# Seven block products in place of eight in the gate/up part of both feed-forward layers

## The reference, cut to what matters

```python
D_FF = 2816                                 # ((8 * 1024 + 3 * 256 - 1) // (3 * 256)) * 256

def swiglu(h, w_gate_up, w_down):
    gu = h @ w_gate_up                      # (tokens, 1024) @ (1024, 5632)
    g, u = gu[..., :D_FF], gu[..., D_FF:]
    return (jax.nn.silu(g) * u) @ w_down    # (tokens, 2816) @ (2816, 1024)

x = x + mix
x = x + swiglu(rms_norm(x, norm_ffn_g[i]), w_gate_up[i], w_down[i])
```

## Time and profile before

| | |
|---|---|
| device time, median of 3 runs | 1802.62 us (1800.88 to 1804.29) |
| the profiled execution | 1802.11 us |
| its span | 1800.4 us |
| mean granted TensorE clock | 0.997 of full |
| PE busy | 97% |
| VectorE busy | 46% |
| ScalarE busy | 34% |
| GpSimd busy | 2% |

### The profile page before, as it was taken

How to read it: one execution, slowest core, us unless ns; L and a number is a source line. 1 busy time by engine, 2 the same in 40 slices (tenths; PEclk the granted TensorE clock), 3 DMA queues, 4 the chain that set the end, 5 groups by cost and what they waited for, 6 DMA issues and landing times.

```text
span 1800.4 us, 33060 instructions
## 1 busy us (share of the span) xinstructions
PE 1747.0 (97%) x14564; PEld 1622.8 (90%) x14564; DVE 827.6 (46%) x975; ACT 610.6 (34%) x887; POOL 28.1 (2%) x51
## 2 busy tenths in 40 slices
PE   7999999999999999999999998999899999999999
PEld 7999666689999999999999995666899999999999
DVE  6663366664433333334532327777544423442333
ACT  5443355553221122112342206666442211221221
POOL 0000000000000000000000000000000000000000
PEclk9999999999999999999999999999999999999999
DMA  5225799921222222112223339998122222122122
GB/s 187 74 96 205 288 378 381 376 101 65 94 70 71 74 91 70 71 71 72 92 94 129 129 118 373 374 375 318 71 71 72 92 71 71 70 72 93 71 70 82
DMA packets 38436, 258.42 MB, mean 144 GB/s; under 512 B 4528, under 2 KB 4656, under 8 KB 9264
## 3 DMA queue, kind: packets, MB, share of 16 engines
q1 hardware_dynamic: 34560, 245.15, 36.7%
q0 software_dynamic: 3760, 11.54, 1.8%
HBM read 242.51 MB, written 13.11 MB: 142 GB/s over the span
## 4 chain that ended last, share of the span: by engine, by line
PE 89%; DVE 5%; ACT 3%; issue 2%; DMA 0%; SPq 0%; ACTq 0%; DVEq 0%
PE ps L412 62%; PE ps L212 4%; PE ps L213 4%; PE ps L214 4%; PE ps L768 3%; PE ps L672 2%; PE ps L719 2%; PE ps L688 2%; PE ps L455 2%; PE ps L701 1%; PE ps L676 1%; PE ps L739 1%; DVE pw L1035 1%; ACT sp L892 1%; DVE st L1055 1%
## 5 line engine op out<-in xcount | busy, mean ns | idle before, releaser
L412 PE MATMUL ps<-h_hi,w_hi 128*128 128x320 f32 x1664 | 380.1, 310 | 2.6 <-DVE qks L1277 1.1
L412 PE MATMUL ps<-h_hi,w_lo 128*128 128x320 f32 x1664 | 379.2, 309 | 0.0
L412 PE MATMUL ps<-h_lo,w_hi 128*128 128x320 f32 x1664 | 379.0, 309 | 0.0
L190 DVE TENSOR_TENSOR w_lo<-w_raw,w_hi 128x2048 fp32r<-128x2048 f32 x99 | 226.8, 2291 | 154.1 <-ACT w_hi L182 144.3
L412 PEld LDWEIGHTS ps<-h_hi,w_hi 128*128 128x128 f32 x1664 | 278.2, 188 | 3.7 <-DVE w_lo L190 2.5
L412 PEld LDWEIGHTS ps<-h_lo,w_hi 128*128 128x128 f32 x1664 | 278.2, 188 | 0.0
L182 ACT ACTIVATE w_hi<-w_raw 128x2048 fp32r<-128x2048 f32 x99 | 188.7, 1906 | 263.7 <-PE ps L412 263.5
L412 PEld LDWEIGHTS ps<-h_hi,w_lo 128*128 128x128 f32 x1664 | 278.0, 188 | 0.0
L212 PE MATMUL ps<-w_hi,h_hi 128*128 128x256 f32 x640 | 183.0, 286 | 11.8 <-DVE h_lo L243 10.6
L213 PE MATMUL ps<-w_lo,h_hi 128*128 128x256 f32 x640 | 181.8, 284 | 0.0
L214 PE MATMUL ps<-w_hi,h_lo 128*128 128x256 f32 x640 | 181.7, 284 | 0.0
(11 more groups left out here) (186 smaller groups left out, 2098.2 us busy)
## 6 DMA issues: line engine op xcount, KB each, us to landing
w_raw<-in_w SPq DMA_DIRECT2D x99, 1024.0 KB, 4.8
kv<-in_k_s SPq DMA_DIRECT2D x30, 1024.0 KB, 8.2
kv<-in_v_a SPq DMA_DIRECT2D x18, 1024.0 KB, 7.9
work<-in_v_s SPq DMA_DIRECT2D x16, 1024.0 KB, 8.8
kv<-in_k_a SPq DMA_DIRECT2D x14, 1024.0 KB, 8.6
work<-in_v_a SPq DMA_DIRECT2D x14, 1024.0 KB, 8.8
extra<-in_k_a SPq DMA_DIRECT2D x8, 1024.0 KB, 7.4
w_raw<-in_k_a SPq DMA_DIRECT2D x8, 1024.0 KB, 8.9
```

The costliest lines, as they stand in the source:

```text
L190: nc.vector.tensor_tensor(w_lo[s][:, :, :], w_raw[:, s, :, :], w_hi[s][:, :, :].bitcast(F32), ALU.subtract).then_inc(lo_done, 1)
L412: last = nc.tensor.matmul(ps[:, bank0 + 2 * n + h, 0:HALF], w[:, k, n * P:(n + 1) * P], m[:, k, h * HALF:(h + 1) * HALF], start=(k == 0 an ...
```

## The change

Both feed-forward layers compute gate and up of one block with Strassen's algorithm in Winograd's form. The factors are taken as 2 x 2 blocks: the tokens in two halves, the 8 input tiles as 4 pairs of an even and an odd tile, the outputs as gate and up. Seven products of 4 input tiles by 320 tokens by 128 outputs replace eight. A product is 4 x 3 = 12 matmuls of the size used before, and a unit 84 of them in place of 96. The down units are as before.

The operands of the products are sums of blocks. On the token side they are made once per layer (class `PairNorm`: ScalarE, VectorE, and on GpSimd `difference` and `add`, which also sums the squares). On the weight side three of the seven are blocks of `w_raw` and four are sums, which GpSimd makes for every unit (`factor13`, `factor4`). The high and low parts of the seven are made one by one (`gu_hi_block`, `gu_lo_block`), each as soon as the product before that used its buffer is done. The results are combined through three PSUM banks a unit: a bank is read, and then a further product is accumulated onto it. GpSimd also takes three of the elementwise operations behind a unit. The loops of the feed-forward layers are written out.

```diff
+            def begin(i):
+                pe.wait_ge(lo_done, split_count(g, j, i))
+                if i < 3:
+                    if v > 1:
+                        pe.wait_ge(ff[("g0", "c21", "c12")[i]], v - 1)
+                else:
+                    pe.wait_ge(ff[("p1", "u2", "p5", "u3")[i - 3]], v + 1)
+            def product(i, pairs):
+                (w1, w0), (m1, m0) = (s_hi[i], s_lo[i]), combos(i)
+                for p in pairs:
...
+                    for a, (w, m) in enumerate(((w1, m1), (w1, m0), (w0, m1))):
+                        last = nc.tensor.matmul(ps[:, bank[i], 0:HALF], w[:, p, :], m[:, p, :],
+                                                start=(i < 3 and p == 0 and a == 0), stop=(p == 3 and a == 2),
...
+            def factor13(g, j, v):
+                raw_ready(pool, g, j, j % 2)
+                if v > 0:
+                    pool.wait_ge(lo_done, gu_split(v - 1, 4))
...
+                nc.gpsimd.tensor_tensor(out, b0[:, 512:1536], b0[:, 0:1024], ALU.subtract).then_inc(ff["t"], 1)
+                pool.wait_ge(ff["t"], 3 * v + 1)
+                nc.gpsimd.tensor_tensor(t2[:, :, :], raw_block(j % 2, 2), t13[:, 0], ALU.subtract)\
...
+                    if j > 0:
+                        gate_half(v + j - 1, 1 - s)
+                    if j + 1 < n:
+                        factor4(g, j + 1, v + j + 1)
+                    if j > 0:
+                        scale(v + j - 1, 1 - s)
+                    up_half(v + j, s)
+                    if j + 2 < n:
+                        factor13(g, j + 2, v + j + 2)
...
+                    copy_p1(act, v + j, s)
+                    if more:
+                        gu_hi_block(act, g, j + 1, 0)
+                    if j > 0:
+                        silu(v + j - 1, 1 - s)
+                    if more:
+                        gu_hi_block(act, g, j + 1, 1)
+                    copy_p5(v + j, s)
+                    if more:
+                        gu_hi_block(act, g, j + 1, 2)
+                        gu_hi_block(act, g, j + 1, 3)
+                    else:
+                        split_hi(act, d, 0, 0, (prod, 7 * (v + n) - 3))
+                    if j > 0:
+                        split_gu(v + j - 1, j - 1)
...
+            def u3(v, s):
+                dve.wait_ge(prod, 7 * v + 5)
+                nc.vector.tensor_tensor(up[:, s, HALF:TOK], ps[:, 3 * s + 1, 0:HALF], p1[:, s, :], ALU.add)\
...
+                    if more:
+                        gu_lo_block(dve, g, j + 1, 0)
+                    u2(v + j, s)
+                    if more:
+                        gu_lo_block(dve, g, j + 1, 1)
+                        gu_lo_block(dve, g, j + 1, 2)
+                    if j > 0:
+                        product(v + j - 1, 1 - s)
+                    g0(v + j, s)
+                    if more:
+                        gu_lo_block(dve, g, j + 1, 3)
+                    u3(v + j, s)
+                    if not more:
+                        split_lo(dve, d, 0, 0)
+                    else:
+                        gu_lo_block(dve, g, j + 1, 4)
+                    if j > 0:
+                        split_gu(v + j - 1, j - 1)
+                    c12(v + j, s)
+                    if more:
+                        gu_lo_block(dve, g, j + 1, 5)
+                    c21(v + j, s)
+                    if more:
+                        gu_lo_block(dve, g, j + 1, 6)
```

More of the change, by code:

```diff
@@ L157, in program, with layer @@
         settled = sem("settled")
[L160 to L164, removed]
+        def layer(f):
+            for c, n in enumerate(CHUNKS):
+                yield from ((f"g{f}{c}", n, 0, 7), (f"d{f}{c}", 4, 2, 1))
+        order = [("qkv", 12, TT, 1), ("oa", 4, 2, 1), *layer(0), ("ks", 4, 2, 1), ("vs", 4, TT, 1), ("qb", 4, 2, 1),
+                 ("ob", 4, 2, 1), *layer(1)]
+        units, splits, u0, m0 = {}, [], 0, 0
+        for name, n, per, parts in order:
+            l0 = splits[-1] if splits else 0
+            units[name] = (u0, m0, per, l0, parts)
+            splits += [l0 + parts * (j + 1) for j in range(n)]
             u0, m0 = u0 + n, m0 + n * per
@@ L436, in program @@
         x_done = sem("x_done")
[L438 to L445, removed]
+        OUT = (6, 4)
         def output_pe(pe, ph, x0, ready, ready_s, mid=None):
-            pe.wait_ge(lo_done, units[ph][0] + 1)
+            pe.wait_ge(lo_done, split_count(ph, 0))
             for h in range(2):
@@ new lines, in pair_act, with pair_dve, chunks @@
+        def pair_act(f):
+            nm = norms[f"ffn{f}"]
+            return lambda act, j: nm.pair_act(act, j, (lambda: copy_p1(act, f * N_F, 0)) if j == 3 else None)
+        def pair_dve(norm):
+            return lambda dve, j, n: norm.odd_dve(dve, j) if n else norm.even_dve(dve, j)
+        ff = sems("ff", "t p1 p5 u2 u3 g0 c12 c21 c22 g1 silu sr gu hi lo")
+        prod = sem("prod")
+        N_F = sum(CHUNKS)
+        def chunks(f):
+            v = f * N_F
+            for c, n in enumerate(CHUNKS):
+                yield c, n, f"g{f}{c}", f"d{f}{c}", v
+                v += n
@@ new lines, in ffn_pe @@
+        def ffn_pe(pe, f, x0, nm):
+            for c, n, g, d, v in chunks(f):
+                for j in range(n):
+                    gu_unit(pe, g, j, v + j, nm if c == 0 and j == 0 else None)
+                v += n
+                for j in range(4):
+                    frees = [[(x_done, x0 + 2 * j - 1)], [(x_done, x0 + 2 * j)]]
+                    if j == 0:
+                        frees[1] += [(ff["c21"], v), (ff["c12"], v)]
+                    feature_unit(pe, d, j, j % 2, gu_hi, gu_lo, n, OUT, frees,
+                                 [(ff["lo"], v - 1)] if j == 0 else (), [(ff["lo"], v)] if j == 0 else ())
+                x0 += KT
```

573 lines of the change are left out of this document (430 added, 143 removed).

## The result

| | before | after |
|---|---|---|
| median of 4 runs, us | 1803.21 (1800.88 to 1804.29) | 1783.93 (1783.19 to 1784.52) |
| profiled execution / its span, us | 1802.11 / 1800.4 | 1783.48 / 1781.7 |
| matmuls | 14564 | 14036 |

The ratio is 0.9895, with a 95% interval of [0.9877, 0.9912]: 19 us faster, where 71 were forecast. The time lies in the range given, but a quarter of the gain arrived.

What follows compares the result with a forecast made beforehand. TensorE's matmuls were taken to bound the kernel: 1802.1 - 77.4 removed + 7.5 edges - 0.9 removed wait = 1731.3, 1732 us for the median. Range 1722 to 1848; 1722 to 1747 for the forecast case alone, chance 0.48.

Steps and rivals of the forecast that it cites:

- What bounds the kernel: Feed-forward layers: TensorE's matmuls, 146.7 ns apart, set the time; removing them gains their time until another engine can't follow.
- the removed 77.4 us: 44 gate/up units lose 12 matmuls each, 528 in all at 146.7 ns: 77.4 us less.
- No dearer matmuls: Gate/up products: a matmul whose weights differ from the previous one's costs nothing extra, so 146.7 ns stays.
- gaps within a product: Rival, gate/up products: more waits open gaps in the matmul stream; 0.25 us a product gives 1808; chance 0.05.
- A steady unit loses nothing.: Steady gate/up units: other engines follow in 12.32 us, u3 0.7 us early, so the whole 77.4 us is gained.
- GpSimd's price: GpSimd's six two-input operations of a gate/up unit: between 3.4 and 9.0 us, worked with at 9.0.
- The rival Exclusion: Gate/up units: two-input SBUF operations of VectorE and GpSimd never overlap; unit floor 9.9 to 15.5 us, mostly 1800 to 1875; chance 0.30.
- Partial slowing: Rival, gate/up units: VectorE and GpSimd lengthen each other without excluding, 1.2 us a unit, 1778, range 1747 to 1800; chance 0.17.
- The Trainium skill's estimate: Gate/up units, from two documentation pages: GpSimd 7.3 us, both engines together 13.8 us a unit, total 1789.
- The edges: Chunk ends and layer starts: longer tails and late operands add 7.5 us together, between 0 and 15.
- Chunk ends: First down unit waits 0.45 us at 6 ends, 2.7 us; its last k 1.1 us late twice, 2.2 us.
- The layer starts: Each feed-forward layer's second unit: u3 ready at 25.3, due at 24.0, 1.3 us late, twice, 2.6 us.

Runs made afterwards that it cites:

- experiment 2: Changed kernel with GpSimd's six two-input operations of a unit replaced by MEMSETs of about the same length: 1729.68 us, 0.9601 of the kernel before.
- experiment 6: Changed kernel with g0, the fourth low part and u3 ahead of VectorE's product, and ScalarE's fifth high part ahead of gu_hi: 1783.60 us.
- the small program: Separate program, computing nothing of the reference, timing VectorE and GpSimd operations apart and side by side in ten stretches; VectorE's ten low parts alone took 6.11 us.
- 9: Changed kernel, steady units' GpSimd work on VectorE, first unit's u3 earlier; GpSimd keeps token work and weight sums of each chunk's first two units: 1741.62 us.

## Why the prediction was wrong

- **What bounds the kernel, and the removed 77.4 us**: right. With VectorE never blocked by GpSimd in a unit (experiment 2) the profiled execution is 1729.6: 77.4 removed and 4.9 added in all, where the prediction had 6.6 net. No dearer matmuls and no gaps within a product. One reading was loose without harm: the piece of 3168 matmuls begins 48 matmuls into the layer, behind the norm's four, and ends 48 into the next stage; the distance of 146.7 ns stands.
- **The failed step: "A steady unit loses nothing."** It kept 0.69 us for VectorE's low part and looked only whether GpSimd's results come in time. The low part's mean became 1188 and 1392 ns, and the unit 13.69 us instead of 12.32; 40 of the 52 us that are missing stand there. The chain was to have `scale` done 6.6 us and u3 9.9 us into the unit. In the unit that TensorE began at 508.86, `scale` ends at 9.0 us (517.88) and u3 at 11.7 (520.57): "0.7 us early" became 1.1 late.
- **GpSimd's price**: bounded by 3.4 and 9.0 us, worked with at 9.0; it is 7.5 as turns. Inside, and the forecast didn't fail on it: as a duration without contention even 9.0 was affordable.
- **The rival Exclusion** had the mechanism, with the signs that were named for it: spans stretched by the other's length, no two at a time, TensorE waiting for L921. Its sizes were off in two places that partly cancel. VectorE's share of the turns is 5.30 us, not 6.5 (operations that follow each other start 0.61 and 0.74 apart, and 0.55 is left after a wait), so the floor is 12.8. But GpSimd's round begins after u3, which adds 0.89. By the rival's formula 7.5 us would give a unit of 14.0 and 1796. Its argument against itself, that GpSimd has nothing to do while VectorE works towards u3, doesn't hold as it was meant: `scale` was there until 9.0 us, and the 2.76 us for which GpSimd then does stand idle are no relief, as it waits in them for u3 and the round is that much longer. As it priced itself mostly above 1800, this time fell where Partial slowing had been put, whose mechanism is not what the rows show. In that rival's own sum `factor4` stands at 8.8, behind the silu, for which it doesn't wait; behind `gate_half` it would be 8.1.
- **The Trainium skill's estimate**, 7.3 us for GpSimd, both engines 13.8 us a unit and 1789 in all, was the nearest number in the prediction, 5 us off. Part of that is luck: it took 57 us for the steady units, which lost 40, and 7.5 for the edges, which took 21. The rule behind it is what the rows show; it got 0.30, since no row of before showed the two engines together; no row spoke against it either.
- **The edges**: 7.5 us forecast, 17.9 measured, and 3.1 more for the half clock, on which the prediction has no term. Chunk ends 5.8 + 2.3 against 2.7 + 2.2. The layer starts were put at 1.3 us in the second unit; it is 3.2 in the first, for want of the GpSimd queue: 2.01 us of square sums, then 4.5 us of weight sums. In experiment 2 the same place cost 1.1 us of idle time, so some two thirds of this stop come from GpSimd's longer operations and their turns.
- **Still open**: how far the steady unit can be brought towards 12.80 with all six operations left on GpSimd, if its round did not start with u3. It wasn't tried. Nor is it shown by a run of its own that the 0.89 us of g0, u3 and the start are what separates 13.69 from 12.80: they close the count in the one unit that was read, and experiment 6 fits.

## What to carry to other kernels

Before you give GpSimd a share of VectorE's work, add up both engines' operations on SBUF that exclude each other, as if one engine did them, and compare the sum with the unit's time; then look for the closed round through both queues, whose waits come on top. Here six operations that cost 7.50 us of turns a unit on GpSimd took 4.4 us on the already busier VectorE, and the kernel became 42 us faster, with a changed order in the first unit that was worth 2.5 at most. An experiment with MEMSETs in place of the suspected engine's reads separates the blocking from the order in one run.

## What the runs showed of the hardware

- The exclusion isn't limited to two inputs on GpSimd: six one-input copies of 1024 columns took VectorE's ten low parts from 6.11 to 11.17 us. VectorE's fp32 copy with one SBUF input was drawn out too, from 0.41 to 2.56 us beside a GpSimd operation of 1024 columns.
- While both engines have such work they take turns one by one, neither twice in a row, as the ends in the unit show. For ten low parts against eight GpSimd operations of 512 columns the sum is 6.11 + 8 x 1.16 = 15.4 us; it took 14.67.
- A low part that has waited takes 0.55 us more after the other's end (0.54 to 0.56 in the unit, 0.55 in the small program), where its record alone is 0.69 and its distance from the one before 0.61.
- VectorE's operations with an input in PSUM beside GpSimd (6.07 against 6.11 us), GpSimd's MEMSETs beside VectorE (6.11) and ScalarE's copies beside GpSimd (9.26 for GpSimd's four, as beside PSUM readers) met nothing.
- Behind a stop of 3.0 us TensorE's granted clock was 0.50 for 3.41 us in both layers of after, and every matmul of 320 columns 267 ns from the next instead of 147; no such stretch lies there in experiments 2 and 9, whose stops at the seventh product were 1.1 and 1.3 us.
